# Products of one-hots in two float32r passes instead of one float32 product

## The reference, cut to what matters

```
idx, gate = ...                       # T x 128: chosen experts (i * 128 + j), softmax weights
act = gelu(einsum('tkd,td->tk', expert_u[idx], x))
out = einsum('tk,tkd->td', gate * act, expert_v[idx])
```

## Time and profile before

| | us |
|---|---|
| median of 3 runs | 3463.15 (3463.12 to 3464.73) |
| the profiled execution | 3457.04 |
| its span, first to last instruction | 3455.3 |
| PE busy in the span | 3269.0 (95%) |
| DVE busy | 2551.4 (74%) |
| ACT busy | 910.8 (26%) |

### The profile page before, as it was taken

How to read it: one execution, slowest core, us unless ns; L and a number is a source line. 1 busy time by engine, 2 the same in 40 slices (tenths; PEclk the granted TensorE clock), 3 DMA queues, 4 the chain that set the end, 5 groups by cost and what they waited for, 6 DMA issues and landing times. The chain is left out here.

```text
span 3455.3 us, 46046 instructions
## 1 busy us (share of the span) xinstructions
PE 3269.0 (95%) x17804; PEld 2870.0 (83%) x17804; DVE 2551.4 (74%) x5345; ACT 910.8 (26%) x1319; POOL 800.3 (23%) x626
## 2 busy tenths in 40 slices
PE   6999989799999999989999999968999999999996
PEld 5867755499999999989999999966888888888884
DVE  4621253421499999988988898847899898998995
ACT  3210300211122222224444444411222222222222
POOL 0000000000001111113333333323344344443441
PEclk8999989899999999999999999988999999999998
DMA  3020021311144444448888889779888888888883
GB/s 96 14 39 27 13 92 55 116 44 43 62 133 145 146 139 145 146 157 289 294 320 295 327 290 334 277 274 316 301 299 303 301 298 298 299 305 301 300 294 128
DMA packets 339553, 695.58 MB, mean 201 GB/s; under 512 B 40956, under 2 KB 201528, under 8 KB 333176
## 3 DMA queue, kind: packets, MB, share of 16 engines
q1 hardware_dynamic: 255192, 386.29, 33.1%
q0 software_dynamic: 84144, 306.35, 26.0%
HBM read 580.11 MB, written 110.64 MB: 200 GB/s over the span
## 5 line engine op out<-in xcount | busy, mean ns | idle before, releaser
L1725 POOL DMA_INDIRECT dr_row<-in_peer_v_dram,idx x288 | 427.7, 1485 | 662.8 <-DVE acc_s L1744 636.5
L1725 POOL DMA_INDIRECT gr_row<-in_peer_u_dram,idx x240 | 290.5, 1210 | 482.1 <-DVE raw L1734 463.6
L1744 DVE SCALAR_TENSOR_TENSOR acc_s<-dr_row,gate,acc_s 128x1024 f32<-128x1024 f32 x288 | 367.2, 1275 | 0.0
L2271 DVE TENSOR_TENSOR acc<-pd_po,acc 128x512 f32<-128x512 f32 x384 | 264.0, 688 | 116.5 <-PE pd_po L2304 116.5
L1734 DVE CUSTOM_DVE_ANT_0 gr_row<-gr_row,xs 128x1024 f32<-128x1024 f32 x240 | 287.6, 1217 | 2.6 <-DMA gr_row<-in_peer_u_dram,idx 2.6
L2157 ACT ACTIVATE pg_wb<-pg_pw 128x512 f32<-128x512 f32 x192 | 207.9, 1102 | 51.7 <-PE pg_pw L2135 48.9
L476 PE MATMUL fr_a<-pj_w,h_t 128*128 128x256 f32 (+1 forms) x864 | 198.1, 391 | 16.2 <-PEq L176 16.2
L2108 DVE TENSOR_SCALAR pg_hot_i<-pg_iota,sel_t 128x128 f32<-128x128 f32 x768 | 212.9, 354 | 0.0
L476 PEld LDWEIGHTS fr_a<-pj_w,h_t 128*128 128x128 f32 (+1 forms) x864 | 170.1, 226 | 43.3 <-issue 21.4
L2135 PE MATMUL pg_pw<-pg_hot_i,pg_hot_j 128*128 128x128 f32 x1536 | 200.6, 276 | 3.0 <-DVE pg_hot_i L2108 3.0
L2135 PEld LDWEIGHTS pg_pw<-pg_hot_i,pg_hot_j 128*128 128x128 f32 x1536 | 192.7, 192 | 3.4 <-DVE pg_hot_i L2108 3.4
(11 more groups left out here) (479 smaller groups left out, 7935.2 us busy)
## 6 DMA issues: line engine op xcount, KB each, us to landing
pd_v<-in_peer_v_dram SPq DMA_DIRECT2D x128, 512.0 KB, 4.8
w_d<-pg_wb SPq DMA_DIRECT2D x48, 1024.0 KB
pd_w<-w_d SPq DMA_DIRECT2D x64, 768.0 KB, 7.1
pd_a<-act_d SPq DMA_DIRECT2D x64, 768.0 KB
ta_u<-in_peer_u_dram SPq DMA_DIRECT2D x64, 512.0 KB
ga_u<-in_peer_u_dram SPq DMA_DIRECT2D x64, 512.0 KB
act_d<-ta_a SPq DMA_DIRECT2D x128, 192.0 KB
act_d<-ga_a SPq DMA_DIRECT2D x128, 192.0 KB
```

Of the source, the lines that this page charges most:

```text
L1725: pool.indirect_dma_start(self.buf[i % self.n][:], None, self.table, bass.IndirectOffsetOnAxis(ap=self.idx[:, col:col + 1], axis=0)).then_ ...
L1744: self.nc.vector.scalar_tensor_tensor(out=out, in0=self.buf[i % self.n][:], scalar=w[:, col:col + 1], in1=out, op0=ALU.mult, op1=ALU.add). ...
L2271: nc.vector.tensor_tensor(out, po[(OUTS * g + o) % NPO][:], out, ALU.add).then_inc(o_added, 1)
```

## The change

The gate product is made in two float32r products instead of one float32 product. gate is rounded to float32r by ScalarE (`g_hi`), in two halves of 384 tokens, and VectorE works out ratio = (gate - g_hi) / g_hi in four operations of 128 x 384 for each half (`split`): the first half ahead of all one-hots, the second after group 1. VectorE writes hot_j and hot_h into float32r buffers (the exact 0/1 matrix, and the 0/gate matrix rounded); ScalarE scales hot_h by ratio of the token into hot_l, four activations for each group (`weigh`). TensorE multiplies hot_j by hot_h into the bank, then the previous group's hot_j by its hot_l onto that group's bank (`small_part`), and only then is that group done. ScalarE's copy to `wb` (`store`) is that of the previous group, behind `weigh` of this one. The ring of hot buffers goes from 4 to 3, that of PSUM banks from 2 to 4, that of gathered rows from 5 to 4.

```diff
-NHB = 4
+NHB = 3
-        hot_i = sb("hot_i", [P, NHB, BT, P])
-        hot_j = sb("hot_j", [P, NHB, BT, P])
+        hot_h, hot_l, hot_j = (sb(f"hot_{x}", [P, NHB, BT, P], F32R) for x in "hlj")
+        g_hi = sb("g_hi", [P, TD // 2], F32R)
+        ratio = sb("ratio", [P, TD])
-        rows_u = Rows(ctx, nc, "gr", u_d, idx, ROWS_TOPK, NR, 5)
-        pw = [ctx.enter_context(nc.psum_tensor(f"pg_pw{b}", [P, BT, P], F32)) for b in range(2)]
+        rows_u = Rows(ctx, nc, "gr", u_d, idx, ROWS_TOPK, NR, 4)
+        pw = [ctx.enter_context(nc.psum_tensor(f"pg_pw{b}", [P, BT, P], F32)) for b in range(4)]
...
+            def split(half):
+                own = slice(half * TD // 2, (half + 1) * TD // 2)
+                dve.wait_ge(g_rounded, half + 1)
+                high = g_hi[:].bitcast(F32)
+                nc.vector.tensor_tensor(ratio[:, own], sel_t[:, 2, own], high, ALU.subtract).then_inc(split_step, 1)
+                nc.vector.tensor_scalar(high, high, 1e-30, None, ALU.max).then_inc(split_step, 1)
+                dve.wait_ge(split_step, 4 * half + 2)
+                nc.vector.reciprocal(high, high).then_inc(split_step, 1)
+                dve.wait_ge(split_step, 4 * half + 3)
+                nc.vector.tensor_tensor(ratio[:, own], ratio[:, own], high, ALU.mult).then_inc(split_step, 1)
+                dve.wait_ge(split_step, 4 * half + 4)
+                dve.sem_inc(g_split, 1)
+            split(0)
             for s in range(STEPS + 2):
                 if s < STEPS:
                     for g in groups_at(s):
                         one_hots(g)
+                        if g == 1:
+                            split(1)
...
+            def small_part(g):
+                pe.wait_ge(small, g + 1)
+                for j in range(BT):
+                    mm = nc.tensor.matmul(pw[g % 4][:, j, :], hot_j[:, g % NHB, j, :], hot_l[:, g % NHB, j, :],
+                                          start=False, stop=True, skip_group_check=True)
+                mm.then_inc(made, 1)
...
                     pe.wait_ge(hot, g + 1)
-                    if g >= 2:
-                        pe.wait_ge(stored, g - 1)
+                    if g >= 4:
+                        pe.wait_ge(stored, g - 3)
                     for j in range(BT):
-                        mm = nc.tensor.matmul(pw[g % 2][:, j, :], hot_j[:, g % NHB, j, :], hot_i[:, g % NHB, j, :],
-                                              start=True, stop=True)
-                    mm.then_inc(made, 1)
+                        nc.tensor.matmul(pw[g % 4][:, j, :], hot_j[:, g % NHB, j, :], hot_h[:, g % NHB, j, :],
+                                         start=(j == 0), stop=False, skip_group_check=True)
+                    if g >= 1:
+                        small_part(g - 1)
+                    if g == BANKS - 1:
+                        small_part(g)
...
+            def weigh(g):
+                act.wait_ge(hot, g + 1)
+                act.wait_ge(g_split, 1 if (g + 1) * BT <= TD // 2 else 2)
+                for j in range(BT):
+                    tok = slice(g * BT + j, g * BT + j + 1)
+                    ins = nc.scalar.activation(hot_l[:, g % NHB, j, :], hot_h[:, g % NHB, j, :].bitcast(F32), ACT.Copy,
+                                               scale=ratio[:, tok])
+                ins.then_inc(small, 1)
...
+            for half in range(2):
+                if half == 1:
+                    act.wait_ge(g_split, 1)
+                nc.scalar.activation(g_hi[:], sel_t[:, 2, half * TD // 2:(half + 1) * TD // 2], ACT.Copy).then_inc(g_rounded, 1)
             for s in range(STEPS):
                 for g in groups_at(s):
+                    weigh(g)
+                    if g >= 1:
+                        store(g - 1)
+                    if g == BANKS - 1:
+                        store(g)
```

More of the change, by code:

```diff
@@ L2043, in peer_gates @@
         iota = sb("iota", [P, P])
-        hot_i = sb("hot_i", [P, NHB, BT, P])
-        hot_j = sb("hot_j", [P, NHB, BT, P])
+        hot_h, hot_l, hot_j = (sb(f"hot_{x}", [P, NHB, BT, P], F32R) for x in "hlj")
+        g_hi = sb("g_hi", [P, TD // 2], F32R)
+        ratio = sb("ratio", [P, TD])
         wb = [sb(f"wb{b}", [P, NK, WCH]) for b in range(2)]
         up = Up(ctx, nc, "ga", UP_TOPK, u_d, act_d, h, 2)
-        rows_u = Rows(ctx, nc, "gr", u_d, idx, ROWS_TOPK, NR, 5)
-        pw = [ctx.enter_context(nc.psum_tensor(f"pg_pw{b}", [P, BT, P], F32)) for b in range(2)]
-        shaped, hot, made, stored = sem("shaped"), sem("hot"), sem("made"), sem("stored")
+        rows_u = Rows(ctx, nc, "gr", u_d, idx, ROWS_TOPK, NR, 4)
+        pw = [ctx.enter_context(nc.psum_tensor(f"pg_pw{b}", [P, BT, P], F32)) for b in range(4)]
+        shaped, hot, small, made, stored = sem("shaped"), sem("hot"), sem("small"), sem("made"), sem("stored")
+        g_rounded, g_split, split_step = sem("g_rounded"), sem("g_split"), sem("split_step")
         wrote = [sem(f"wrote{b}") for b in range(2)]
@@ L2107, in one_hots @@
                     tok = slice(g * BT + j, g * BT + j + 1)
-                    ins = nc.vector.tensor_scalar(hot_i[:, hb, j, :], iota[:], sel_t[:, 0, tok], sel_t[:, 2, tok],
+                    ins = nc.vector.tensor_scalar(hot_h[:, hb, j, :], iota[:], sel_t[:, 0, tok], sel_t[:, 2, tok],
                                                   ALU.is_equal, ALU.mult)
                 ins.then_inc(hot, 1)
+            def split(half):
[11 more added lines that the diff above has]
+            split(0)
             for s in range(STEPS + 2):
@@ L2148, in _, with store @@
         def _(act):
+            def weigh(g):
[6 more added lines that the diff above has]
+                ins.then_inc(small, 1)
+            def store(g):
+                c, t0 = g // BC, g % BC * BT
+                if c >= 2 and t0 == 0:
+                    act.wait_ge(wrote[c % 2], 16 * PIECES * (c // 2))
+                act.wait_ge(made, g + 1)
+                nc.scalar.activation(wb[c % 2][:, :, t0:t0 + BT].rearrange("p i t -> p t i"), pw[g % 4][:],
+                                     ACT.Copy).then_inc(stored, 1)
             for half in range(2):
                 up.high(act, 0, half)
+            for half in range(2):
+                if half == 1:
+                    act.wait_ge(g_split, 1)
+                nc.scalar.activation(g_hi[:], sel_t[:, 2, half * TD // 2:(half + 1) * TD // 2], ACT.Copy).then_inc(g_rounded, 1)
             for s in range(STEPS):
                 for g in groups_at(s):
[L2153 to L2158, removed]
+                    weigh(g)
[3 more added lines that the diff above has]
+                        store(g)
                 n, k = s // 3, s % 3
```

## The result

The changed kernel takes 3493.95 us (median of 4 runs, 3492.53 to 3497.17) against 3463.14: ratio 1.009, 95% interval 1.0073 to 1.0108. The predicted time was 3493. The profiled execution took 3497.17 us, its span 3495.4. That is 40 us above the profiled one of before, where the medians are 31 apart, as the profiled execution of before lies 6 us under its median and this one 3 above. The stage itself, from that load to the first product of the next stage, takes 847.2 us instead of 812.5: +34.7.

What follows compares the result with a forecast made beforehand. TensorE, busy 696.44 of 700 us in the stage, was taken as the bound. Products 0, waits for hot_l 20, last group 2 and start 8 gave +30 on 3463.15, so 3493 us, range 3466 to 3525.

Steps and rivals of the forecast that it cites:

- The passes: Gate products on TensorE: 1536 float32r records at the same distance as the float32 ones, 0 us (bounds -6 to +14).
- max(streaming, load): Distance between float32r records of 128 columns on TensorE: the larger of 0.065 streaming and 0.11 weight load, so 0.11 to 0.112.
- The slope of the wider products: From float32r products of 288 and 384 columns: 0.041 us for 96 columns, giving 0.065 at 128 if streaming sets pace.
- The waits for hot_l: TensorE waits in steps with two groups: 6 x (0.55 in k = 0, 0.9 in k = 1, 1.9 in k = 2), 20 us.
- The last group: Stage's end: last group weighed and added in the same step behind another, about 2 us.
- The start: Stage's start: split(0) ahead of the one-hots delays the first product 3.9 us; with split(1) together +8 us (bounds 4 to 10).
- split(1): VectorE, ahead of group 2: takes 3.9 us again, counted nearly in full at 3.7.
- The clock: TensorE's granted clock, read as 1.00 in the kernel before; no term for it in the sum.
- The ring of gathered rows: Four gathers in flight give 12 us on average, some 8.8 at the tightest, against 6.0 landing: 0, at most +5.
- The ring of hot buffers: Three hot buffers: VectorE can begin a group at least one long step ahead, 3 us covering 0.685 + 1.1 of work: 0.
- rival (c): VectorE becomes the bound, 50 us more if tensor_scalars writing float32r take longer (420 ns, not 354): 3515 us, chance 0.15.
- Rival (b): ScalarE's queue has more slack than counted, steps with two groups are absorbed, only the start remains: 3470 us, chance 0.10.

Runs made afterwards that it cites:

- b_two: Kernel before with float32r hot buffers and each product issued twice, without the gate's remainder, ScalarE work or split: 3461.77 us, ratio 1.0007.
- a_bf: Changed kernel with hot_l products after up products, splits moved behind one-hots, bfloat16 hot buffers, four hot and five gathered-row buffers: 3437.89 us, ratio 0.9937.
- a_defer: Changed kernel reordered: hot_l products behind the step's up products, ScalarE weighs first, then stores the previous step's groups; nothing left out: 3473.45 us, ratio 1.0038.
- b_rings: Kernel before with only the smaller rings: 3 hot buffers instead of 4, 4 gathered-row buffers instead of 5: 3459.27 us, ratio 1.0.
- a_best5: Changed kernel with hot_l products after up products, first split behind group 0's one-hots, second spread, five gathered-row buffers: 3468.95 us, ratio 1.003.
- a_nosplit: Changed kernel without rounding and splits, ratio a constant 2^-13 written by GpSimd, the four activations kept: 3487.84 us, ratio 1.0072.
- a_oneact: Changed kernel with one constant-scale activation per group instead of four, so the remainder is not computed: 3478.39 us, ratio 1.0046.

## Why the prediction was right

The sum was +30; the medians are 31 apart, and the stage of the profiled executions grew by 35.

**The passes: 0, measured 0 (-0.4 by the distances of b_two, 1.0007 by its time).** The step that decided the sign was max(streaming, load) with the load read from two loads that started 0.11 us apart. b_two and a_bf both confirm it, one by the time and by the pair of products that are 0.06 apart, the other by halving the load and with it the distance. The slope of the wider products, 0.065, was nearly the true streaming price and the wrong one for the sum.

**The waits for hot_l: 20, measured 17, and 1.2 in the next steps.** Which steps wait, and in which order, came out as worked: none with one group but the six behind k = 1, 0.62 where I had 0.55, and for k = 2 weigh's end at the 3.2 us of the prediction, though the want comes 0.3 later than I had it, mostly as TensorE waits 0.23 for hot_h first. For k = 1 I had 0.9 and it is 0.62 and 0.2 in the next step. Reading ScalarE's queue instruction by instruction was worth it: ScalarE is only 70% busy and still sets the pace in 18 steps of 192.

**The last group: 2, measured 1.5. The start: 8, measured 5.7 to 6.8.** split(0) was 4.1 us against 3.9 (the reciprocal 2.55 against 2.4, by 6 ns for each element). split(1) was the term of wrong size: 3.7 predicted, 1.5 measured, as the lead of the one-hots that I had left out of account was half there.

**The clock: 0, measured about 11.** This is the step that the prediction lacks. I costed a wait at its length. Behind the seven waits of 1.3 to 1.5 us TensorE was granted the 1.2 GHz level in six stretches of 3.4 us or 6.8. That the total came out as predicted is therefore partly luck: of these 11 us and the 2.6 of short waits, the smaller start and the shorter waits for hot_l made room for 6, and the loads for 3. In a_defer, with those waits gone, the stretches are gone.

**The covers.** The ring of gathered rows 0, confirmed by b_rings and a_best5. The ring of hot buffers was put at 0 too, with 3 us of cover; the trace lays 1.4 us to it, the short waits for hot_h in the six k = 2 steps with two groups. Tensor_scalar 355 ns, which ends rival (c), as does VectorE's 617 of 700. Rival (b) had the double steps absorbed; a_nosplit, at 1.0072 without any split, shows that they are not. VectorE does wait more: 59.8 us for products, which the ring of three holds back. Nearly all of it costs nothing, since TensorE's own waits for hot_h are the start and those 1.4 us.

## What to carry to other kernels

A float32r product with 128 moving columns and new weights costs the load of its weights, 0.111 us, and two of them cost what a float32 product costs; here the split paid only when both parts were bfloat16, whose loads take half. Where the moving side is wide the load is hidden and the split should pay: a float32 product with 256 columns takes 0.43 us, a float32r one with 288 takes 0.133. No run here tries that. When one engine is full, read the queue of whoever feeds it in the fullest step, not its mean share: a helper at 70% cost some 29 us through 19 waits and the clock behind seven of them, and the same instructions in another order gave 18 back. Work that is saved on the full engine is got only up to the next floor, so look first how much of it the loads and the helpers would let through: here some 30 us of 85, twice.

## What the runs showed of the hardware that I had not expected

- In the changed kernel five waits of TensorE of 1.45 us were each followed by 3.4 us at a granted clock of 0.51 to 0.54, which cost 1.6 us more; a sixth, with one of 1.34 right behind it, by 6.8 us, 2.7 more. The length of the wait alone doesn't decide it: in a_oneact a wait of 2.42 us for a load (at 1938.61) left the clock at 1.00, and one of 0.72 us did not. What does wasn't settled.
- With its weights loaded ahead a float32r product of 128 columns takes 0.06 us, and 0.111 when each load has to be waited for. bfloat16 weights of 128 columns load in 0.056 us, float32r ones in 0.111.
- A reciprocal of 384 columns takes VectorE 2.55 us, where the subtract of the same size takes 0.55.
- Behind the last gate record an up product starts after 0.03 us if the gate product is float32 and after 0.11 if it is float32r. Behind a transpose a gate record starts after 0.11 if it is float32 and after 0.03 if it is float32r. Over the stage the distances come out even.
